# Last expert of a routed feed-forward: its predecessor's down product between gate and up, the output normalized beside the last product, the last rows finished on chip and stored by index

## What is computed

```python
def expert_choice_ffn(h, w_router, w_gate, w_up, w_down):
    cap = EC_CAPACITY_FACTOR * n // N_EXPERTS            # 128 of 1024 tokens
    aff = jax.nn.softmax((h @ w_router).astype(jnp.float32), axis=-1)
    g, idx = lax.top_k(jnp.swapaxes(aff, 1, 2), cap)
    xs = jax.vmap(lambda hb, ib: hb[ib])(h, idx)
    a = jnp.einsum('becd,edf->becf', xs, w_gate)
    u = jnp.einsum('becd,edf->becf', xs, w_up)
    y = jnp.einsum('becf,efd->becd', jax.nn.silu(a) * u, w_down) * g[..., None].astype(h.dtype)
    out = jax.ops.segment_sum(y.reshape(-1, d), flat, num_segments=bsz * n)
    ...
x = x + gt2 * expert_choice_ffn(h2, w_router[l], w_gate[l], w_up[l], w_down[l])
return rmsnorm_2(x, g_final)
```

## Time and profile before

| | us |
|---|---|
| median of 3 runs | 2768.28 (2768.26 to 2769.24) |
| the profiled execution | 2771.62 |
| its span | 2770.1 |
| busy PE, DVE, ACT, POOL | 2554.7, 1496.3, 913.3, 178.0 |
| chain that ended last, shares of the span | PE 83%, DVE 11%, ACT 2%, DMA 1%, issue 1%, POOL 1% |
| all transfers | 370.02 MB, mean 134 GB/s |

### The profile page before, as it was taken

How to read it: one execution, slowest core, us unless ns; L and a number is a source line. 1 busy time by engine, 2 the same in 40 slices (tenths; PEclk the granted TensorE clock), 3 DMA queues, 4 the chain that set the end, 5 groups by cost and what they waited for, 6 DMA issues and landing times.

```text
span 2770.1 us, 30328 instructions
## 1 busy us (share of the span) xinstructions
PE 2554.7 (92%) x12043; PEld 2041.0 (74%) x12043; DVE 1496.3 (54%) x1913; ACT 913.3 (33%) x1501; POOL 178.0 (6%) x224
## 2 busy tenths in 40 slices
PE   6999899999999999999998899999944999999993
PEld 5786578888887777787787777898843666666771
DVE  5998734333535554444448414665467656665542
ACT  4234524432412111211134211432342544554431
POOL 1001300000000000000101000000000000000001
PEclk9999899999999999999999999999966999999997
DMA  4111021400113223222223011101163899999975
GB/s 139 61 39 42 31 114 38 152 32 8 61 46 99 77 99 92 98 83 91 76 91 114 31 62 35 43 1 66 76 248 114 321 362 360 370 367 372 365 269 197
DMA packets 114006, 370.02 MB, mean 134 GB/s; under 512 B 6214, under 2 KB 11382, under 8 KB 113905
## 3 DMA queue, kind: packets, MB, share of 16 engines
q1 hardware_dynamic: 90128, 284.71, 27.6%
q0 software_dynamic: 23776, 83.90, 9.6%
HBM read 343.37 MB, written 25.26 MB: 133 GB/s over the span
## 4 chain that ended last, share of the span: by engine, by line
PE 83%; DVE 11%; ACT 2%; DMA 1%; issue 1%; POOL 1%; DVEq 0%; ACTq 0%; POOLq 0%
PE banks L404 21%; PE banks L406 21%; PE banks L405 21%; PE banks L2160 8%; DVE conv_out L1284 3%; PE banks L2103 2%; DVE w_lo L398 2%; PE banks L484 1%; PE banks L2093 1%; PE banks L2079 1%; PE banks L2084 1%; PE banks L1966 1%; PE banks L1945 1%; ACT w_hi L391 1%; DVE top_index L1703 1%
## 5 line engine op out<-in xcount | busy, mean ns | idle before, releaser
L1737 DVE TENSOR_TENSOR expert_w_lo<-expert_w,expert_w_hi 128x2048 fp32r<-128x2048 f32 x128 | 287.0, 2285 | 222.1 <-ACT expert_w_hi L1172 221.9
L404 PE MATMUL banks<-act_hi,w_hi 128*128 128x512 f32 x960 | 378.0, 394 | 12.1 <-DVE act_lo L498 5.6
L405 PE MATMUL banks<-act_lo,w_hi 128*128 128x512 f32 x960 | 375.7, 391 | 0.0
L406 PE MATMUL banks<-act_hi,w_lo 128*128 128x512 f32 x960 | 375.5, 391 | 0.0
L1172 ACT ACTIVATE expert_w_hi<-expert_w 128x2048 fp32r<-128x2048 f32 x128 | 237.5, 1905 | 174.8 <-DMA expert_w<-in_w_gate 76.4
L391 ACT ACTIVATE w_hi<-w_raw 128x1024 fp32r<-128x1024 f32 x152 | 156.4, 1060 | 353.4 <-PE banks L406 353.3
L398 DVE TENSOR_TENSOR w_lo<-w_raw,w_hi 128x1024 fp32r<-128x1024 f32 x152 | 181.0, 1222 | 166.5 <-ACT w_hi L391 162.4
L404 PE MATMUL banks<-w_hi,act_hi 128*128 128x512 f32 (+1 forms) x640 | 248.5, 388 | 14.3 <-DVE rotated L1563 5.8
L406 PE MATMUL banks<-w_hi,act_lo 128*128 128x512 f32 (+1 forms) x640 | 245.5, 384 | 0.0
L405 PE MATMUL banks<-w_lo,act_hi 128*128 128x512 f32 (+1 forms) x640 | 245.5, 384 | 0.0
L2160 PE MATMUL banks<-expert_w,expert_hidden_T 128*128 128x512 f32 x512 | 222.7, 593 | 2.3 <-DMA expert_w<-in_w_down 1.2
(11 more groups left out here) (324 smaller groups left out, 3944.7 us busy)
## 6 DMA issues: line engine op xcount, KB each, us to landing
expert_w<-in_w_gate SPq DMA_DIRECT2D x32, 2048.0 KB, 9.8
expert_w<-in_w_up SPq DMA_DIRECT2D x32, 2048.0 KB, 10.2
expert_w<-in_w_down SPq DMA_DIRECT2D x32, 2048.0 KB, 7.9
ada_w<-in_w_ada POOLq DMA_DIRECT2D x48, 512.0 KB, 4.1
w_raw<-in_mlp_up_w SPq DMA_DIRECT2D x16, 1024.0 KB, 5.4
w_raw<-in_mlp_down_w SPq DMA_DIRECT2D x16, 1024.0 KB, 5.0
w_raw<-in_w_in SPq DMA_DIRECT2D x14, 1024.0 KB, 5.4
w_raw<-in_w_out SPq DMA_DIRECT2D x8, 1024.0 KB, 5.1
```

Source lines behind the costliest of these rows:

```text
L404: nc.tensor.matmul(o_, lh, rh, start=start, stop=False)
L405: nc.tensor.matmul(o_, lh, rl, start=False, stop=False)
L406: return nc.tensor.matmul(o_, ll, rh, start=False, stop=stop)
L1737: dve.tensor_tensor(EWL[slot][:, c, :], EW[slot][:, c, :], EWH[slot][:, c, :], ALU.subtract).then_inc(w_ready, 1)
```

## The change

On TensorE the tail of the last two experts is written out in another order: gate of expert 15, down of expert 14, up of expert 15, the transposes, and the down product of expert 15. That last one goes through the whole contraction for the first 512 output columns and then for the second 512, and gives `ex_d` once for each half.

The scatter of expert 14 is now the last one that adds to `expert_sums`. Behind it SP loads all eight tiles of the sums into `final_rows` (`XB`, in the place of gate weights), counting on the semaphores `x_in`, and POOL gathers the 128 rows of expert 15's tokens from the same sums into `last_rows` (`XZ`). ScalarE and VectorE normalize the eight tiles, SP stores them. VectorE then makes the gated result of expert 15 in two halves, adds it to `last_rows`, and these 128 rows are normalized by a ninth step of the same kind (`8 + NT`). POOL waits until the eight stores have landed and stores the 128 rows over them by index, without adding.

The last expert's result no longer passes through `expert_sums`, and its addition is on VectorE and not in the transfer.

```diff
@@ -267,6 +267,9 @@
     HTE = at("expert_hidden_T", [P, 8, P], F32, O_R + 56 * K + 512)
     YE = at("expert_out", [P, D], F32, O_R + 60 * K + 512)
     GT2 = at("gate_row2", [P, D], F32, O_R)
+    XB = at("final_rows", [P, NT, D], F32, O_RAW)
+    JB = at("final_squares", [P, D], F32, O_WL)
+    XZ = at("last_rows", [P, D], F32, O_WL + 4 * K)
 
 
     PAIR = [nc.alloc_psum_tensor(f"banks{2 * i}{2 * i + 1}", [P, 1024], F32) for i in range(4)]
@@ -505,11 +508,11 @@
         def a_lo(t):
             return AL[:, :, tok(t)]
 
-        def plain_stats(j, src):
+        def plain_stats(j, src, junk=JUNK):
 
             if j >= 1:
                 nc.scalar.wait_ge(pl_sd, j)
-            nc.scalar.activation(JUNK[:, :], src, ACT.Square, accum_out=SS[:, 44 + j:45 + j]).then_inc(pl_sq, 1)
+            nc.scalar.activation(junk[:, :], src, ACT.Square, accum_out=SS[:, 44 + j:45 + j]).then_inc(pl_sq, 1)
             nc.scalar.wait_ge(pl_sq, j + 1)
             nc.scalar.activation(SD[:, 44 + j:45 + j], SS[:, 44 + j:45 + j], ACT.Sqrt, bias=EPSC[:, 0:1],
                                  scale=1.0 / D).then_inc(pl_sd, 1)
@@ -605,6 +608,8 @@
                                      "down", "out", "gate_col"))
         fin_out = sem("final_out")
 
+        BULK, BULK_COUNT = x_in, [32] * NT
+
         block = stack.enter_context(nc.Block())
 
 
@@ -685,6 +690,12 @@
                     load_expert(e - 1, 2, half, when=e - 1)
             for half in range(2):
                 load_expert(NE - 1, 2, half, when=NE - 1)
+            sp.wait_ge(y_out, 16 * (NE - 1))
+            for t in range(NT):
+                sp.dma_start(XB[:, t, :], acc_d[tok(t), :]).then_inc(BULK[t], 16)
+            for t in range(NT):
+                sp.wait_ge(pl_x, 8 + t + 1)
+                sp.dma_start(out[0, tok(t), :], XB[:, t, :]).then_inc(fin_out, 16)
             sp.wait_ge(fin_out, 16 * NT)
 
         @block.gpsimd
@@ -844,18 +855,19 @@
                     gather(e + 3)
                 if e < 0:
                     continue
+                if e == NE - 1:
+                    pool.indirect_dma_start(XZ[:, :], None, acc_d[:, :], bass.IndirectOffsetOnAxis(ap=GI[:, e:e + 1], axis=0)).then_inc(xs_in, 16)
+                    continue
                 pool.wait_ge(ex_y, e + 2)
 
                 pool.indirect_dma_start(acc_d[:, :], bass.IndirectOffsetOnAxis(ap=GI[:, e:e + 1], axis=0), YE[:, :], None,
                                         compute_op=ALU.add).then_inc(y_out, 16)
                 pool.wait_ge(y_out, 16 * e + 16)
                 pool.sem_inc(y_free, 1)
-            for t in range(NT):
-                pool.dma_start(X[:, t, :], acc_d[tok(t), :]).then_inc(x2_in[t], 16)
-            for t in range(NT):
-                pool.wait_ge(pl_x, 8 + t + 1)
-                pool.dma_start(out[0, tok(t), :], X[:, t, :]).then_inc(fin_out, 16)
             pool.wait_ge(fin_out, 16 * NT)
+            pool.wait_ge(pl_x, 8 + NT + 1)
+            pool.indirect_dma_start(out[0], bass.IndirectOffsetOnAxis(ap=GI[:, NE - 1:NE], axis=0), XZ[:, :], None).then_inc(y_out, 16)
+            pool.wait_ge(y_out, 16 * NE)
 
 
         @block.scalar
@@ -1206,8 +1218,10 @@
             expert_act(NE - 1, more=False)
 
             for t in range(NT):
-                act.wait_ge(x2_in[t], 48)
-                plain_stats(8 + t, X[:, t, :])
+                act.wait_ge(BULK[t], BULK_COUNT[t])
+                plain_stats(8 + t, XB[:, t, :], JB)
+            act.wait_ge(ex_y, NE + 2)
+            plain_stats(8 + NT, XZ[:, :], JB)
 
 
         @block.vector
@@ -1761,12 +1775,23 @@
             expert_dve(0, first=True)
             with dve.Fori(1, NE - 1) as e:
                 expert_dve(e)
-            expert_dve(NE - 1, more=False)
-            expert_y(NE)
-
+            expert_y(NE - 1)
+            expert_hidden(NE - 1)
+
+            dve.wait_ge(ex_y, NE)
+            dve.tensor_copy(GVC[:, :], GV[:, NE - 1:NE]).then_inc(ex_gv, 1)
+            dve.wait_ge(ex_gv, NE)
             dve.wait_ge(gain_in, 80)
             for t in range(NT):
-                plain_rows(8 + t, X[:, t, :])
+                plain_rows(8 + t, XB[:, t, :])
+            dve.wait_ge(xs_in, 16 * NE + 16)
+            for half in range(2):
+                cols = slice(512 * half, 512 * (half + 1))
+                dve.wait_ge(ex_d, NE + half)
+                dlink(dve.scalar_tensor_tensor(out=YE[:, cols], in0=PAIR[2][:, cols], scalar=GVC[:, 0:1], in1=GT2[:, cols],
+                                               op0=ALU.mult, op1=ALU.mult))
+                dve.tensor_tensor(XZ[:, cols], XZ[:, cols], YE[:, cols], ALU.add).then_inc(ex_y, 1)
+            plain_rows(8 + NT, XZ[:, :])
 
 
         @block.tensor
@@ -2210,10 +2235,22 @@
                 rows_T(e + 1)
                 down(e)
                 hidden_T(e, e + 2)
-            gate_up(NE - 1)
+            pe.wait_ge(ex_xl, NE)
+            pe.wait_ge(ex_sg, NE - 1)
+            split_product(0, 0, NE - 1, ex_g, ew_half[0])
             down(NE - 1)
+            pe.wait_ge(ex_he, NE - 1)
+            split_product(1, 2, NE - 1, ex_u, ew_half[1])
             hidden_T(NE - 1, NE)
-            down(NE)
+            pe.wait_ge(ex_hc, NE)
+            pe.wait_ge(ex_y, NE)
+            for half in range(2):
+                for k in range(8):
+                    if half == 0 and k % 4 == 0:
+                        pe.wait_ge(ew_in[4 + k // 4], 16 * (NE - 1) + 16)
+                    m = pe.matmul(BK[4 + half][:, :], HTE[:, k, :], EW[4 + k // 4][:, k % 4, 512 * half:512 * (half + 1)],
+                                  start=(k == 0), stop=(k == 7))
+                m.then_inc(ex_d, 1)
 
 
 NAMES = ["x", "mem", "positions", "norm_mix_w", "w_in", "conv_w", "conv_b", "conv_ln_w", "conv_ln_b", "ret_gn_w", "w_out",
```

## The result

The changed kernel takes **2746.93 us** (median of 4 runs, 2746.22 to 2748.52). The kernel before, run beside it, takes 2768.76 us (4 runs, 2768.26 to 2771.06). The ratio is 0.9923, with a 95% interval of 0.9908 to 0.9938: 21.8 us or 0.77% faster. The forecast was 2748.5 us and 19.8 us less. The profiled execution took 2748.52 us, its span is 2746.9 us.

A forecast was written before the change was run, and what follows sets the result against it. A serial tail without a full engine was taken as the bound; covering eight tiles with matrix work brings the span from 2770.1 to 2750.3, 19.8 us less, so 2768.28 - 19.8 = 2748.5 us; range 2744.5 to 2755.

The forecast's parts named there:

- Order on TensorE: TensorE's tail: expert 14's down product moves behind expert 15's gate, ending at 2701.35; last product starts at 2715.80, 1.6 us later.
- The last product: Expert 15's down product on TensorE: from 2715.80 to 2729.55, 13.75 us, without the 1.17 us wait for weights.
- rival (d): TensorE's clock falls before the last product: 2 us later at no cost; whole product at half clock 2758.6 us, chance 0.03.
- sign of being right: On TensorE, the last product would run from about 2715.8 to 2729.5 with a granted clock of 1.00.
- Scatter: Expert 14's accumulating scatter from POOL: issued at 2703.0, landed 9.5 us later beside a load of down weights.
- Tiles: Eight tiles on ScalarE and VectorE, beside the last down product: from 2716.5, 15.25 us as before, done at 2731.75.
- Last rows: Last 128 rows on VectorE behind the eighth tile: halves and additions 3.0 us to 2734.75, normalized by 2737.85.
- Hand-over to POOL: From the last scaled rows to POOL's issue of the indirect store: 0.28 us, at 2738.15.
- Stores: POOL's wait for eight landed stores: 8.9 MB at 390 GB/s, landed 2738.4; a tie with the 2738.15 issue, nothing added.
- sign of being wrong: At the end of the tail, POOL would wait for the stores and not for the last rows.
- Indirect store: POOL's final store of 128 rows by index: 4.3 us to landing, at 2742.45, after the fastest indirect read.
- Closing: Closing work between the last store's landing and the end of the span: 7.85 us, as before.

The follow-up runs named there:

- e6: Changed kernel with expert 15's down weights loaded into the place of its gate weights, so no weight load runs beside expert 14's scatter; 2746.86 us.
- the repeat: The unaltered changed kernel profiled and timed once more, beside the version with all edits on the same chip; 2746.82 us, tail 60.97 us.
- e5: Changed kernel with nine matmuls that nobody reads put into TensorE's gaps before the last product; 2746.68 us.
- e4_stores_twice: Changed kernel with each of the eight tiles stored a second time, into scratch rows; 2756.84 us.
- e7: Changed kernel with the edits of e5 and e6, plus ScalarE's early root table load and first tile ahead of its copy; 2744.39 us, again 2743.89 us.
- e8: e7 without the nine unread matmuls; 2744.75 us, ratio 0.9917 against the kernel before.

## Why the prediction was right

All times are us behind the silu's start, 2687.64 in the prediction's frame and 2684.80 in the trace.

- **Order on TensorE.** Down product of expert 14 ends: predicted 13.71, measured 2698.50 - 2684.80 = 13.70. Last product starts: 28.16, measured 28.17. The stretch of waits from up to the product was foreseen to 0.01 us, since every part of it had a row.
- **The last product** was to take 13.75 us and took 15.70. (13.75 is a step of the chain; in the timeline, where 15.70 stands, expert 14's product takes 13.89, so 1.8 us are the lower clock.) The size was missed, and the mechanism stood as rival (d): a granted clock of 0.63 over four us, as after the last product of before, and an end 2 us later without cost. The chance of 0.03 was for the expensive form only, a whole product at half clock; that did not come. The prediction's own sign of being right, a granted clock of 1.00, failed all the same.
  The Trainium skill, page TensorE: Matmul & The Clock Gate, section Part 1, has half the clock as the default that activity lifts; the fall behind idle time and its absence with the gap filled agree in direction.
- **Scatter.** Issued 15.36, measured 15.35; landed in 9.5, measured 9.7. That the slow value is the right one beside a weight load is shown by e6 (6.2 without it).
- **Tiles.** First square 28.86, measured 28.81; done 44.1, measured 2729.07 - 2684.80 = 44.27. They had the cover: one wait of 0.28 us.
- **Last rows.** Added 47.1, measured 2731.83 - 2684.80 = 47.03; scaled 50.2, measured 50.05. Durations of 0.75 and 0.69 us as in the earlier trace rows.
- **Hand-over to POOL.** 0.28 us, read from a plain store of before. For the indirect store it is 0.82: mis-sized by 0.54.
- **Stores.** Called a tie between the stores' landing (50.76, by bytes) and the last rows (indirect store issued 50.5, so 0.25 us apart). Measured: landed 51.16, issued 51.42, 0.55 us behind what the last rows would allow (50.05 + 0.82 = 50.87); in the repeat 50.25, no loss. A tie is what came; that POOL waited for the stores in the first trace was named as a sign of being wrong, and is worth 0.55 us. Rate predicted 390 GB/s, measured (383 + 408 + 320 + 420) / 4 = 383 from 2712 to 2728.
- **Indirect store.** Landed in 3.4 us, predicted 4.3 by the indirect read. The choice of the nearest row failed: a store by index is nearer to the plain store (2.9) than to a read by index. It is 3.4 in the changed kernel and in all nine runs that have such a store.
  The Trainium skill, page DMA: Bandwidth & Descriptors, section Anatomy of one DMA, has a formula for a DMA by its bytes; worked out for 512 KB, an estimate of 3.2 us. It was nearer to the measured 3.4 than the row that the prediction took.
- **Closing.** 7.85 us predicted, 2746.9 - (2736.22 + 3.4) = 7.28 measured. Why it is shorter is not shown.

The sum: 62.66 predicted, 62.10 measured. Against the terms as predicted, the indirect store goes out 0.9 us later (0.54 of the hand-over, 0.55 of the stores, less 0.16 for rows that were ready earlier), lands 0.9 us faster, and the closing is 0.6 shorter. The mechanism and all terms up to the last rows hold; that the misses behind them nearly cancel is luck. The forecast of 19.8 us held with 20.4 by the first trace and 82.46 - 60.97 = 21.5 by the second; the medians give 21.8.

## What to carry to other kernels

A serial strand at the end of a kernel is cut by finding work that depends on all but a small part of the result, running it beside the last matrix work, and redoing it for the small part alone; here neither the new order (2.0 us lost) nor the split (9.8 gained) says what both give (20.4). Write down the second limit under each one: where three strands (product, tiles, transfers) ended within 2 us of each other, the edits of e5 and e6 to one of them showed nothing, and they showed something only together with a third. When a product is moved behind its own inputs, look for idle stretches ahead of it on TensorE: here the granted clock fell behind two of 1.37 and 1.11 us, and by the traces this was paid as soon as the slack behind the product was gone.

## What was not expected

- **The start varies.** The kernel before and e4_stores_twice reach the silu of expert 15 at 2687.64 and 2687.91, all the others between 2683.20 and 2685.45. Much of the difference is made in the first 90 us, far from any edit: at that point the changed kernel's trace is 2.98 us ahead of before, e4's level with it, the others 0.9 to 2.9 ahead, and some gain up to 2.5 us more later. From 40 to 60 us the granted clock is 0.91 in the first two and 1.00 in the others, but five of the others have 0.69 to 0.73 from 20 to 40 us, so the clock alone does not sort them. The windows of before and of the changed kernel:

```profile
40.00:60.00 20.00, 17.66 (x80) 14.50 (x79) 6.46 (x14) 7.07 (x12) 0.00 (x0) 0.91 0.00 0
```

```profile
40.00:60.00 20.00, 17.66 (x87) 14.65 (x86) 7.98 (x17) 6.01 (x9) 0.00 (x0) 1.00 0.00 0
```

  What decides which way an execution takes stays open; it was not tried. It is 3 us, more than most of the differences between the experiments, and the reason for measuring tails.
- **Store by index as cheap as a plain one.** 3.4 us to landing in every run that has it, against 2.9 for a plain store and 6.1 to 6.3 for the accumulating one with nothing beside it. So the index alone is not what makes the accumulating scatter slow. Whether it is the adding up is not shown, since the two also write to different tensors.
- **Nine unread matmuls** (1.29 + 1.17 us of TensorE) bring back 1.7 us of a product, with the end of the program 1.7 us earlier in e7 than in e8 by the tails, while the medians, 2744.39 and 2744.75, don't tell the two apart.
